# Three buffers for the high parts of peer_u, and transposes issued one unit earlier

## The reference, cut to what matters

```
u = peer_u[idx]                                   # 16384 experts of 1024 numbers
act = gelu(einsum('thkd,td->thk', u, xb))         # 8 heads x 16 experts for each token
wts = gates * act
out = einsum('thk,thkd->td', wts, peer_v[idx])
```

## Time and profile before

| | us |
|---|---|
| median of 3 runs | 2455.06 (2452.28 to 2457.01) |
| profiled execution | 2455.18 |
| its span, first to last instruction | 2453.4 |

### The profile page before, as it was taken

The page is one execution under the profiler, slowest core; times in us unless marked ns, Lnnn a source line. Parts: engine busy times, 40 slices in busy tenths (PEclk is TensorE's granted clock), DMA queues, the critical chain, the costliest instruction groups (busy, mean ns, idle before and its releaser), DMA issues.

```text
span 2453.4 us, 33207 instructions
## 1 busy us (share of the span) xinstructions
PE 2307.6 (94%) x12935; PEld 1958.8 (80%) x12935; DVE 1534.7 (63%) x2567; ACT 893.1 (36%) x1175; POOL 1130.3 (46%) x554
## 2 busy tenths in 40 slices
PE   6999999959888999999999999999999999999998
PEld 4998899747648987787778878888788888888886
DVE  4766579455722167887899887775555555555552
ACT  3434455561222133323345444455332232222221
POOL 0333246154623246556655765455554444444441
PEclk8999999988998999999999999999999999999999
DMA  7221122647654345555547886686665554455440
GB/s 269 69 87 54 57 72 69 187 139 221 192 189 121 83 121 143 129 154 130 136 131 183 246 249 191 170 216 184 237 229 205 191 202 178 182 204 205 188 154 35
DMA packets 307405, 392.67 MB, mean 160 GB/s; under 512 B 14545, under 2 KB 257637, under 8 KB 302914
## 3 DMA queue, kind: packets, MB, share of 16 engines
q1 hardware_dynamic: 212162, 302.86, 40.5%
q10 hardware_dynamic: 91664, 75.54, 9.5%
q0 software_dynamic: 3456, 12.58, 1.6%
HBM read 305.70 MB, written 81.26 MB: 158 GB/s over the span
## 4 chain that ended last, share of the span: by engine, by line
PE 56%; DVE 4%; POOL 3%; DMA 2%; ACT 1%; issue 1%; ACTq 0%; DVEq 0%
PE bank L2589 28%; PE bank L2046 22%; PE bank L2540 3%; DVE work L2266 2%; POOL utL_hid L2036 2%; DMA work<-sample_rows_dram 1%; DVE work L2269 1%; PE bank L2545 1%; DVE ut_hid L2025 1%; PE bank L2527 1%; POOL work L2224 0%; DVE work L2339 0%; ACT utH_hid L2032 0%; DMA work<-in_peer_u_dram,eu_sm 0%; POOL work L1967 0%
## 5 line engine op out<-in xcount | busy, mean ns | idle before, releaser
L2036 POOL TENSOR_TENSOR utL_hid<-ut_hid,utH_hid 128x1024 fp32r<-128x1024 f32 x128 | 348.0, 2719 | 329.5 <-ACT utH_hid L2032 328.9
L2046 PE MATMUL bank<-pH,utH_hid 128*128 128x512 f32 x1024 | 407.0, 397 | 13.4 <-POOL utL_hid L2036 13.4
L2046 PE MATMUL bank<-pH,utL_hid 128*128 128x512 f32 x1024 | 399.7, 390 | 0.0
L2046 PE MATMUL bank<-pL,utH_hid 128*128 128x512 f32 x1024 | 399.6, 390 | 0.0
L2589 PE MATMUL bank<-area,work 128*128 128x512 f32 x1536 | 350.8, 389 | 0.0
L2589 PEld LDWEIGHTS bank<-area,work 128*128 128x128 f32 x1536 | 288.3, 188 | 59.9
L2025 DVE STREAM_TRANSPOSE ut_hid<-u_hid 128x1024 f32<-128x1024 f32 x128 | 158.8, 1241 | 146.8 <-POOL utL_hid L2036 127.1
L2202 POOL TENSOR_TENSOR pL<-work,pH 128x1024 fp32r<-128x1024 f32 x64 | 155.1, 2423 | 193.8 <-ACT pH L2445 193.7
L824 POOL TENSOR_TENSOR wL_in<-wb_in,wH_in 128x1024 fp32r<-128x1024 f32 x52 | 129.4, 2488 | 243.7 <-ACT wH_in L777 243.7
L864 PE MATMUL ps_in<-hH_in,wH_in 128*128 128x260 f32 x816 | 238.2, 292 | 2.4 <-DVE projarea L915 1.4
L2046 PEld LDWEIGHTS bank<-pH,utH_hid 128*128 128x128 f32 x1024 | 193.0, 188 | 56.5 <-POOL utL_hid L2036 18.7
(11 more groups left out here) (533 smaller groups left out, 4457.8 us busy)
## 6 DMA issues: line engine op xcount, KB each, us to landing
u_hid<-in_peer_u_dram SPq DMA_DIRECT2D x256, 256.0 KB, 5.0
work<-in_peer_v_dram SPq DMA_DIRECT2D x64, 1024.0 KB, 4.9
hidden_dram<-ge_hid ACTq DMA_DIRECT2D x64, 512.0 KB, 3.1
gates_dram<-area ACTq DMA_DIRECT2D x16, 2048.0 KB, 10.3
wb_in<-in_w_in_dram SPq DMA_DIRECT2D x26, 1024.0 KB, 5.3
wstage<-in_w_ada_dram SPq DMA_DIRECT2D x32, 512.0 KB, 4.9
area<-hidden_dram SPq DMA_DIRECT2D x16, 1024.0 KB, 6.8
area<-gates_dram SPq DMA_DIRECT2D x16, 1024.0 KB, 8.7
```

What stands on the lines that cost most here:

```text
L2036: self.nc.gpsimd.tensor_tensor(self.utL[:, u % 2], self.ut[:, u % 2], self.utH[:, u % 2].bitcast(F32), ALU.subtract).then_inc(self.low, 1)
L2046: mm = self.nc.tensor.matmul(self.pa[u % 2][:, :], w[:, u % 2, k, :], x[:, k, :], start=(n == 0), stop=(n == 3 * KD - 1))
```

## The change

`utH` gets a third buffer. `move_high(u)` now writes `utH[u % 3]` and waits, from u = 3, until TensorE has finished unit u - 3. `move_low` and `hide` read that buffer. `utL` keeps two buffers, so `move_low(u)` now waits itself until TensorE has finished unit u - 2, which before was covered by the wait of `move_high`. On ACT, `move_high(1)` is issued between the score evictions 13 and 14, and step u of the loop issues `move_high(u + 2)`. On DVE, `turn(2)` is issued before the loop, after the wait for the scores, and step u issues `turn(u + 3)`. `turn`'s own wait (`low >= u - 1`) and `ut`'s two buffers are unchanged. POOL's and TensorE's order is unchanged. The last stage uses the first two of the three `utH` buffers.

```
-        self.utH = sb("utH", [P, 2, KD, P], F32R)
+        self.utH = sb("utH", [P, 3, KD, P], F32R)
...
     def move_high(self, act, u):
         act.wait_ge(self.turned, u + 1)
-        if u >= 2:
-            act.wait_ge(self.hidden, u - 1)
-        self.nc.scalar.activation(self.utH[:, u % 2], self.ut[:, u % 2], ACT.Copy).then_inc(self.high, 1)
+        if u >= 3:
+            act.wait_ge(self.hidden, u - 2)
+        self.nc.scalar.activation(self.utH[:, u % 3], self.ut[:, u % 2], ACT.Copy).then_inc(self.high, 1)

     def move_low(self, pool, u):
         pool.wait_ge(self.high, u + 1)
-        self.nc.gpsimd.tensor_tensor(self.utL[:, u % 2], self.ut[:, u % 2], self.utH[:, u % 2].bitcast(F32), ALU.subtract).then_inc(self.low, 1)
+        if u >= 2:
+            pool.wait_ge(self.hidden, u - 1)
+        self.nc.gpsimd.tensor_tensor(self.utL[:, u % 2], self.ut[:, u % 2], self.utH[:, u % 3].bitcast(F32), ALU.subtract).then_inc(self.low, 1)
...
             dve.wait_ge(kept, 17)
+            H.turn(dve, 2)
             for u in range(UNITS):
-                if u + 2 < UNITS:
-                    H.turn(dve, u + 2)
+                if u + 3 < UNITS:
+                    H.turn(dve, u + 3)
...
-                if n == 11:
-                    H.move_high(act, 0)
+                if n in (11, 13):
+                    H.move_high(act, (n - 11) // 2)
...
             for u in range(UNITS):
-                if u + 1 < UNITS:
-                    H.move_high(act, u + 1)
+                if u + 2 < UNITS:
+                    H.move_high(act, u + 2)
```

More of the change, by code:

```diff
@@ L2044, in hide @@
         for k in range(KD):
-            for w, x in ((self.utH, self.S.pH), (self.utH, self.S.pL), (self.utL, self.S.pH)):
-                mm = self.nc.tensor.matmul(self.pa[u % 2][:, :], w[:, u % 2, k, :], x[:, k, :], start=(n == 0), stop=(n == 3 * KD - 1))
+            for w, x in ((self.utH[:, u % 3], self.S.pH), (self.utH[:, u % 3], self.S.pL), (self.utL[:, u % 2], self.S.pH)):
+                mm = self.nc.tensor.matmul(self.pa[u % 2][:, :], w[:, k, :], x[:, k, :], start=(n == 0), stop=(n == 3 * KD - 1))
                 n += 1
@@ L2121, in expert_phase @@
         gb = [carve(sc, 2048, (P, NTB, JG, TB)), flat(H.u[1]).rearrange("p (a b c) -> p a b c", b=JG, c=TB)]
-        wH = [carve(sc, 4096, (P, JG, T), F32R), H.utH[:, :, :, :].rearrange("p a k n -> p (a k n)").rearrange("p (a b) -> p a b", b=T)]
+        wH = [carve(sc, 4096, (P, JG, T), F32R), H.utH[:, 0:2, :, :].rearrange("p a k n -> p (a k n)").rearrange("p (a b) -> p a b", b=T)]
         wL = [carve(sc, 6144, (P, JG, T), F32R), H.utL[:, :, :, :].rearrange("p a k n -> p (a k n)").rearrange("p (a b) -> p a b", b=T)]
```

## The result

| | median us (lowest to highest) | ratio to before |
|---|---|---|
| before, 4 runs beside it | 2456.03 (2452.28 to 2461.66) | |
| after, 4 runs | 2507.60 (2506.72 to 2509.48) | 1.0209 [1.0188, 1.0230] |

A forecast was written before the change was run, and what follows sets the result against it. TensorE was taken to bound both halves, only its idle time being winnable. Terms -5.3 + 5 + 33.9 = +33.6 us on 2455.18 gave 2489 us; likeliest case 2470 to 2505, eight in ten runs 2456 to 2514.

The forecast's parts named there:

- the likeliest case: Whole kernel: early transposes close a one-unit loop through POOL and DVE, longer than TensorE's unit; 2489 us, chance 0.56.
- Units 0 to 61, −5.3: First half: unit 12's half of the 10.6 us stall goes, the second comparison's half stays; bounds -10.6 and 0.
- Units 62 to 67, +5: One-quad units: subtraction begins 2.44 us later relative to TensorE, wait met twice; +5 us, bounds 0 and +14.6.
- Units 68 to 121, +33.9: Second half: one-unit loop plus gathers, less head starts, gives 476.5 us against 442.6; bounds 0 and +59.
- The even-odd loop: Units 68 to 121, first quad even, second odd: loop of 7.76 us, 21 units, against TensorE's 7.25.
- The odd-even loop: Units 68 to 121, first quad odd, second even: loop of 7.69 us, 19 units, against TensorE's 7.25.
- less slow: Rival, units 68 to 121: POOL's multiplications and DVE's comparisons run side by side; 25.6 us less, 2463 us, chance 0.15.
- The head start: Units 68 to 121: 1.68 us credited at the end of each of three stretches with gathered rows' matmuls.
- Units 122 to 127, 0: Last units: no gain, POOL's next subtraction still stands behind a low part of `peer_v` that waits for ACT.
- faster: Rival: overlapping links keep the loop shorter than TensorE's unit, leaving only the 10.6 us gain; 2444 us, chance 0.10.
- no change: Rival: something other than the high part sets the subtraction's start, transposes stay where they were; 2455 us, chance 0.07.
- slower still: Rival, units 68 to 121: a held-up comparison pair in one unit of four; +25 us, 2514 us, chance 0.12.

The follow-up runs named there:

- first experiment: Changed kernel with DVE's old transpose order (`turn(u + 2)` at step u, none before the loop), three high buffers and early high parts kept: 2441.06 us, ratio 0.9946.

## Why the prediction held, and where it was off

The forecast was 2489, the time is 2507.6, 18.6 us more: above the 2470 to 2505 that I had given the likeliest case alone, inside the 2456 to 2514 for all. The mechanism is that of the likeliest case. The profiled span grew by 54.3 us where I had 33.6; of the 20.7 us that are missing, 4.1 lie ahead of unit 0, where I had booked nothing. By its steps:

**Units 0 to 61, −5.3; measured −7.0.** Right in kind. TensorE's wait for low parts in this stretch went from 10.1 us in 9 waits to 3.5 in 4 (total, times, longest; before, then changed):

```profile
PE bank L2046 <- POOL utL_hid L2036: 10.1, 9, 1.2
...
PE bank L2048 <- POOL utL_hid L2038: 3.5, 4, 1.0
```

What stays is the second subtraction, as forecast; the timeline of POOL in the changed kernel, first tile's steps 11 and 12:

```profile
935.49 4.36 POOL L2038 TENSOR_TENSOR utL_hid<-ut_hid,utH_hid 128x1024 fp32r<-128x1024 f32 x1 [3.04 <-PE bank L2048]
939.81 1.76 POOL L1967 TENSOR_TENSOR work<-work,work 128x800 f32<-128x800 f32 x1
941.53 5.62 POOL L2038 TENSOR_TENSOR utL_hid<-ut_hid,utH_hid 128x1024 fp32r<-128x1024 f32 x1
```

The first is held up (4.36 us) but started early enough; the second stands behind `pick` and meets the second comparison (941.05 to 944.92). The first experiment shows that the half I had given up was lost to the early transpose too. There DVE's first comparison begins 59.0 us after TensorE's unit 0, here 64.4, a unit later. There the second comparison is the one held up, behind a subtraction that keeps its 2.40 us, and it holds up `pick`; TensorE waits for one low part only (0.5 us) in all its units 0 to 121. DVE and POOL in the first experiment's kernel:

```profile
924.33 3.45 DVE L1962 TENSOR_TENSOR work<-work,iota 128x3200 f32<-128x3200 f32 x1
...
931.31 5.54 DVE L1962 TENSOR_TENSOR work<-work,iota 128x3200 f32<-128x3200 f32 x1
...
931.10 2.40 POOL L2038 TENSOR_TENSOR utL_hid<-ut_hid,utH_hid 128x1024 fp32r<-128x1024 f32 x1 [1.06 <-PE bank L2048]
933.45 5.02 POOL L1967 TENSOR_TENSOR work<-work,work 128x800 f32<-128x800 f32 x1
```

**Units 62 to 67, +5 (bounds 0 and 14.6); measured +20.8.** This is the mis-sized term, 15.8 of the 20.7 us. "I take two" waits of 2.44 was the step that failed: it saw the wait as a delay of the transpose, and not that all of DVE's step stands behind it, `number` included; with `number` moved behind the one-hots 12.1 of the 20.8 go. From the windows, TensorE's idle time grew from 3.4 to 17.5 us, by 14.0, which the upper bound would have held; the other 6.7 are busy time at a lower clock, which no term had. The timeline of TensorE in the changed kernel at unit 63:

```profile
1226.50 2.08 PE L2543 MATMUL bank<-work 128*128 128x128 f32 x8 [7.34 <-DVE work L2271]
...
1228.80 0.63 PE L2048 MATMUL bank<-pL,utH_hid 128*128 128x512 f32 x1
...
1232.47 0.40 PE L2048 MATMUL bank<-pH,utL_hid 128*128 128x512 f32 x1
```

After 7.34 us of idling its matmuls take 0.63 us, one every 0.43, and after 1231.8 us 0.40, one every 0.23. This unit's 24 matmuls took 7.21 us, those of units 65 and 67, after waits of 5.77 and 4.36, took 6.88 and 7.32 instead of 5.45: TensorE came back at the lower of its two levels, 1.2 GHz, each time (at unit 63 the granted clock is 0.50 from 1226.5 to 1231.5 us and 1.00 from 1232.5). The kernel before had one such unit in all (90), the changed one six (89, 92 and 100 besides).

**Units 68 to 121, +33.9; measured +36.4.** The loop is there and nearly as long as worked out. TensorE's own work in these units is, by the earlier trace rows, 40 × 7.25 + 14 × 8.14 + 9 × 1.68 = 419.1 us; the times above that:

| units | number | forecast | measured |
|---|---|---|---|
| even, odd | 11 | 5.6 | 7.7 |
| odd, even | 12 | 5.3 | 2.1 |
| even, odd, even | 4 | 5.5 | 5.7 |
| odd, even, odd | 4 | 7.5 | 4.8 |
| with matmuls of gathered rows | 9 | −4.6 | 1.6 |
| at the gathers (80, 81, 83 to 92, 98, 99) | 14 | 38.1 | 37.9 |
| sum | 54 | 57.4 | 59.9 |

Before, the sum was 23.5. The gathers make most of it. That their sum came out as booked is in part luck: the four at step 90 hold POOL for 4.77 us (1482.88 to 1487.65) where I had 6.02, and units 89, 91 and 92 take about 4.6 us more because TensorE's matmuls in them ran in part at 1.2 GHz, which I had not booked. The timeline of POOL in the changed kernel, step 90, with the first and the last of four gathers:

```profile
1481.68 1.04 POOL L2226 TENSOR_TENSOR work<-work,sel 128x512 f32<-128x512 f32 x1 [4.32 <-DVE work L2268]
1482.88 1.02 POOL L2200 DMA_INDIRECT work<-in_peer_v_dram,eu_sm  x1 [0.16 <-issue]
...
1486.70 0.94 POOL L2200 DMA_INDIRECT work<-in_peer_v_dram,eu_sm  x1 [0.30 <-issue]
1487.65 2.39 POOL L2038 TENSOR_TENSOR utL_hid<-ut_hid,utH_hid 128x1024 fp32r<-128x1024 f32 x1
```

The subtraction follows at 1487.65, DVE's transpose at 1490.14 after 8.54 us of waiting, and unit 91, begun at 1483.69, takes 16.19 us where it took 8.14. The gathers lose nothing in the unit that issues them (unit 90 takes 7.71, the loop's own length), all of it one unit later.

The even-odd loop was given as 7.76 and runs at 7.71 to 7.79 a unit in units 74, 112, 113, 120 and 121; units 68, 72 and 73, right behind the slow stretch, take 8.2 to 8.4. It is the loop of the chain above. The odd-even loop was too long by 0.8. POOL in the changed kernel there:

```profile
1715.30 2.37 POOL L2038 TENSOR_TENSOR utL_hid<-ut_hid,utH_hid 128x1024 fp32r<-128x1024 f32 x1 [0.54 <-PE bank L2048]
1720.20 1.96 POOL L2226 TENSOR_TENSOR work<-work,sel 128x512 f32<-128x512 f32 x1 [2.53 <-DVE work L2268]
1722.54 2.41 POOL L2038 TENSOR_TENSOR utL_hid<-ut_hid,utH_hid 128x1024 fp32r<-128x1024 f32 x1 [0.38 <-PE bank L2048]
```

From 1715.30 to the end of the multiplication at 1722.16 are 6.86 us, not 7.69: I had put DVE's multiplication (0.69) in front of the subtraction, where it isn't. Then POOL waits for TensorE, so this kind takes TensorE's own 7.26 to 7.35 in ten of its twelve units, and its time alone would fit the rival "less slow" too. The 1.96 us are what ruled that rival out: POOL's multiplication is held up behind the second comparison, as the earlier trace rows had the comparison behind the subtraction. So do the even-odd-even units 75 and 83, which take 9.59 us where that rival had 8.14. The 1.96 us also agree with the exclusive lock that the Trainium skill gives in "SBUF — State Buffer", section "SBUF: two separate sides". The head start that I credited to the units behind the gathered rows' matmuls, 1.68 three times, was the error of the other sign: units 98 and 106 used 0.47 of it each (7.29 where the loop takes 7.76).

**Units 122 to 127, 0; measured 0.0.** Subtractions in the stretch before went from 2.72 us on average to 2.46, the fewer collisions that were forecast.

Of the rivals, "faster" is what the kernel does without the early transposes (2441); for "no change" the trace has nothing, and "slower still" (a collision in one unit of four) didn't occur: in units 68 to 121 no comparison took over 1.25 us, where before 19 took 2.0 to 3.5.

## What to carry to other kernels

Ask of a buffer that is to be filled earlier whether it is free earlier. Here it wasn't: the fill's own wait moved forward with it, and everything behind it in the engine's order waited as well. With a third buffer it was free, and the earlier fill then cost nothing and brought nothing. Before such a move, write down the loop (who frees the buffer, what stands behind the fill, who waits for that) and count in how many units it closes; from two units to one is where the slack goes. Move the part of a change that removes a wait by itself: here the high parts alone gave 0.5% and the transposes took 2.6% back.

## What the runs showed of the hardware that was not expected

**Placement.** Moving the high and low parts, with all else behind the work area, by 32, 64 or 128 bytes in each partition made the kernels 20 to 29 us slower, by 512 bytes not. Matmuls of the low parts in 900 to 1200 us (count, busy, mean ns), in the kernel moved by 32 bytes:

```profile
L2048 PE MATMUL bank<-pH,utL_hid 128*128 128x512 f32 x425 | 168.1, 396 | 0.0
```

and in the one moved by 512:

```profile
L2048 PE MATMUL bank<-pH,utL_hid 128*128 128x512 f32 x440 | 171.2, 389 | 0.0
```

Seven ns in each of 24 matmuls are 0.16 us a unit: 5.60 against 5.44 (2.9%), at full granted clock in both. In the kernel moved by 32 bytes the last stage shows it on the moved buffer and not on the other:

```profile
L2591 PE MATMUL bank<-area,work 128*128 128x512 f32 x1298 | 297.0, 389 | 0.0
...
L2591 PE MATMUL bank<-utH_hid,pH 128*128 128x512 f32 x437 | 172.7, 395 | 0.0
```

In `hide` the high and low parts are the weights, in chunks of 512 bytes in each partition, and for its units a rule on the chunk's place within 512 bytes fits all five placements. It doesn't cover the last stage: there the same buffers are the operand of 512 columns, and in the kernel moved by 64 bytes the products of the low parts took 388 ns, as if unmoved, those of the high parts 392 and 394. 256 bytes weren't tried, and which of the moved buffers counts was not separated. The cause stays open.

**The clock after a wait.** In units 62 to 67 of the changed kernel TensorE's waits of 4.4 to 7.3 us were each followed by 4.4 to 5.3 us of work at 1.2 GHz: each wait cost its length, and the products behind it another 1.4 to 1.9 us. In the first experiment's kernel a wait of 4.65 us ahead of unit 63 was followed by 2.9 us at 1.2 GHz, and the products took 0.6 us more. So the price of such a wait can't be read from its length alone.
